# A mixture-of-experts block: routing steps ordered by expert, scatters set between the gathers

## The reference

```python
x = layer_norm(DEEPNORM_ALPHA * x + xa, ln2_g, ln2_b)
scores = sigmoid(x2d @ w_router); sel = scores + router_bias      # 512 x 64
# 8 groups of 8 experts: a group's score is the sum of its top two; keep 4 groups
_, top_idx = lax.top_k(sel, TOP_K)                                # 8 experts per token
w = take_along_axis(scores, top_idx); w = w / w.sum(-1) * ROUTED_SCALE
out = swiglu(x_pad[tok], w_exp_gu[e], w_exp_down[e]) * w          # 64 experts, FF 256
routed + swiglu(x2d, w_sh_gu, w_sh_down)                          # shared expert, FF 256
x = layer_norm(DEEPNORM_ALPHA * x + ff, ln3_g, ln3_b)
```

## Time and profile before

| | us |
|---|---|
| median of 3 runs | 2214.76 (2214.06 to 2220.69) |
| the profiled execution | 2217.79 |
| its span, first to last instruction | 2215.7 |
| PE busy | 2015.8 (91%) |
| DVE busy | 790.7 (36%) |
| ACT busy | 471.6 (21%) |
| POOL busy | 344.0 (16%) |

### The profile page before, as it was taken

One profiled execution on the slowest core, in us unless ns is written; L12 is line 12 of the kernel. 1 busy time (PEld: TensorE's weight loads), 2 busy tenths in 40 slices (PEclk: granted clock), 3 DMA queues, 4 the chain that ended last, 5 costly groups with the idle time before them and its releaser, 6 DMA issues.

```text
span 2215.7 us, 26236 instructions
## 1 busy us (share of the span) xinstructions
PE 2015.8 (91%) x10060; PEld 939.5 (42%) x10060; DVE 790.7 (36%) x1650; ACT 471.6 (21%) x1045; POOL 344.0 (16%) x415
## 2 busy tenths in 40 slices
PE   7888999999977699999999987699988899999997
PEld 3324434445443244443333333344745444444443
DVE  5998771213268033333223222701265300000012
ACT  2235431100300133333333332211244000000000
POOL 0653250000014311111111112400023000000000
PEclk9998999999998799999999999899999999999999
DMA  5110014213222599999999995804310122222210
GB/s 222 47 38 1 10 59 168 76 38 119 110 96 100 193 398 396 403 399 392 391 396 390 392 382 201 316 14 143 124 39 1 63 79 77 76 76 76 76 38 29
DMA packets 67619, 367.91 MB, mean 166 GB/s; under 512 B 11200, under 2 KB 11456, under 8 KB 50784
## 3 DMA queue, kind: packets, MB, share of 16 engines
q1 hardware_dynamic: 44496, 297.76, 35.6%
q10 hardware_dynamic: 10192, 35.57, 4.3%
q0 software_dynamic: 12864, 33.67, 4.2%
HBM read 345.93 MB, written 29.42 MB: 169 GB/s over the span
## 4 chain that ended last, share of the span: by engine, by line
PE 69%; DMA 14%; DVE 10%; issue 4%; POOL 2%; ACT 1%; POOLq 0%; SPq 0%; DVEq 0%; ACTq 0%
PE bank L911 41%; DMA slab<-w_exp_down 12%; PE bank L1231 12%; PE bank L1435 6%; PE bank L920 2%; DVE slab L1846 2%; POOL slot_table L2538 2%; PE bank L1297 2%; DVE slab L1849 1%; PE bank L1249 1%; DVE work L1843 1%; DVE s5x L1846 1%; PE bank L973 1%; DVE slab L1843 1%; PE bank L1193 1%
## 5 line engine op out<-in xcount | busy, mean ns | idle before, releaser
L911 PE MATMUL bank<-slab,ring 128*128 128x512 f32 (+1 forms) x1552 | 660.0, 586 | 13.1 <-DMA ring<-stream 11.4
L911 PEld LDWEIGHTS bank<-slab,ring 128*128 128x128 f32 x1552 | 294.2, 191 | 372.3 <-issue 369.7
L911 PE MATMUL bank<-ring,slab 128*128 128x512 f32 (+1 forms) x608 | 252.8, 576 | 3.9 <-ACT slab L1468 2.1
L1231 PE MATMUL bank<-slab 128*32 128x512 f32 x1536 | 226.1, 593 | 21.3 <-DMA ring<-w_exp_down 15.3
L1231 PE MATMUL bank<-ring,slab 128*32 128x512 f32 x1536 | 227.4, 596 | 18.0 <-DMA slab<-w_exp_down 14.9
L1846 DVE TENSOR_TENSOR slab<-bank,slab 96x256 f32<-96x256 f32 (+3 forms) x120 | 63.8, 531 | 468.8 <-PE bank L911 296.1
L2273 DVE COPY slab<-bank 32x512 f32<-32x512 f32 x124 | 80.9, 688 | 407.6 <-PE bank L1239 407.6
L1239 PE MATMUL bank<-ring,slab 128*32 128x512 f32 x512 | 225.7, 594 | 0.0
L1239 PE MATMUL bank<-slab 128*32 128x512 f32 x480 | 211.6, 594 | 0.0
L2486 POOL TENSOR_TENSOR small<-small 128x1 f32<-128x1 f32 (+2 forms) x30 | 24.0, 801 | 989.9 <-DVE small L1843 989.7
L911 PEld LDWEIGHTS bank<-ring,slab 128*128 128x128 f32 x608 | 115.5, 191 | 137.8 <-issue 129.7
(11 more groups left out here) (263 smaller groups left out, 2185.6 us busy)
## 6 DMA issues: line engine op xcount, KB each, us to landing
ring<-stream SPq DMA_DIRECT2D x173, 512.0 KB, 3.5
slab<-w_exp_gu SPq DMA_DIRECT2D x32, 2048.0 KB
ring<-w_exp_gu SPq DMA_DIRECT2D x32, 2048.0 KB
ring<-w_exp_down SPq DMA_DIRECT2D x32, 1024.0 KB
slab<-w_exp_down SPq DMA_DIRECT2D x32, 1024.0 KB
y_rows<-slab ACTq DMA_DIRECT2D x64, 384.0 KB
gb<-rows ACTq DMA_DIRECT2D x7, 512.0 KB, 5.7
slab<-x_fm SPq DMA_DIRECT2D x1, 2048.0 KB, 9.3
```

The source lines that it names most:

```text
L911: mm = nc.tensor.matmul(dst, lhs[k], rhs[k], start=(k == 0), stop=(k == len(lhs) - 1))
L1231: mm = nc.tensor.matmul(g_bank[32 * g:32 * g + 32, :], x[:, k, 32 * g:32 * g + 32], w[:, 512 * k:512 * k + 512], start=(k == 0), stop=(k = ...
```

## The change

- `psum_order`, `panel_plan`: `pos` before `su` in VectorE's order; the shared down weights leave the ring and come by one DMA of 1 MB into `work` (`sd_w`).
- Norm 2: VectorE normalizes into `xhat` and takes the moments half by half. TensorE transposes `xhat`, rows 0 to 2 as soon as these are done and rows 3 later, and the gain and bias of norm 2 are applied in the copy of the turned tiles, as per-partition scalars. The row form x2, which is stored for the gathers, gets its affine on VectorE for rows 0, 1 (between the halves) and 2 (after the copies), and on GpSimd for rows 3. SP stores it, and loads the rows of norm 3, instead of ScalarE.
- Logits: each 128x64 result in four products with 32 columns of weights, tile by tile as the copies come, for all four row tiles.
- Routing on VectorE: comparisons over all four row tiles at once (128x256), no index search, the rank of a chosen expert within its token by a scan over the chosen mask (so the eight choices of a token come in the order of expert number, not of score), the table address and the y row are one and the same, expert x 96 + slot. For each rank k one fused compare-and-multiply of 128x256 and one reduction give the four addresses of all row tiles.
- The table is laid out by expert. GpSimd scatters rank 0 (four DMAs), then rank k+1 before the gather of expert k, for eight ranks. SP reads the index column of expert e, 96 entries of 4 bytes, by a DMA of its own: for experts 0 to 7 once rank e has been scattered, then in the loop four experts ahead, behind the refills.
- The shared down product comes after the last expert and before the sums.

```diff
@@ SP
-            panels_done(4, 8)
-            gate_up_rows(1, 1)
-            panels_done(8, 10)
-            down_rows(0, 0)
+            def index_column(e):
+                sp.wait_ge(ids_sent[e], 16 * NT)
+                sp.dma_start(slot_tok[:, e % 4:e % 4 + 1], scratch["tab"][e * CAP:(e + 1) * CAP, :]).then_inc(idx_landed[e % 4], 16)
+            sp.dma_start(sd_w, a["w_sh_down"]).then_inc(in_sd, 16)          # after xo
+            early = [(0, 4, lambda: gate_up_rows(0, 0)), (4, 8, lambda: gate_up_rows(1, 1)),
+                     (8, 10, lambda: down_rows(0, 0)), (10, 12, lambda: down_rows(1, 1))]
+            # those whose ring slots hold sg and su (4-8, 8-10) are late, the others go out now
...
+            for t in range(NT):          # wait for x2_dve or x2_pool, then
+                sp.dma_start(scratch["x2"][t * P:(t + 1) * P, :], tm(x2, t)).then_inc(x2_stored, 16)
...
+            down_rows(2, 2)
+            down_rows(3, 3)
+            index_column(0)
+            index_column(1)
+            for x in late:
+                panels_done(*x[:2])
+                x[2]()
             sp.wait_ge(psum_full, plan.full("su", 1))
             gate_up_rows(3, 3)
+            index_column(2)
+            index_column(3)
             for e in range(4):
                 refill(e, e, down=e >= 2)
+                index_column(e + 4)
             with sp.Fori(1, NE // 4 - 1) as u:
                 for b in range(4):
                     refill(4 * u + b, b)
+                    sp.dma_start(slot_tok[:, b:b + 1], scratch["tab"][bass.ds((4 * u + b + 4) * CAP, CAP), :]).then_inc(idx_landed[b], 16)
@@ TensorE
+            for k in range(KD):
+                evac("x2T", k)
+                for t in range(NT):
+                    for g in range(4):
+                        mm = nc.tensor.matmul(tile("lg", t)[32 * g:32 * g + 32, 0:64], fm(x2T, k)[:, t * P + 32 * g:t * P + 32 * g + 32],
+                                              w_rt[:, k, :], start=(k == 0), stop=(k == KD - 1))
...
+                nc.tensor.matmul(dst[:, 0:320], cst("tri"), chosen, start=True, stop=False)
+                for s in range(NT):
+                    n = NT - s
+                    mm = nc.tensor.matmul(dst[:, 64 * s + 64:320].rearrange("p (t e) -> p t e", e=64), ones_f[:, :],
+                                          chosen[:, 64 * s:64 * s + 64].unsqueeze(1).broadcast_to([P, n, 64]),
+                                          start=False, stop=(s == NT - 1))
@@ VectorE
+            link(nc.vector.tensor_tensor_scan(rank, keep_run, chosen[:, 0:256], 0.0, ALU.mult, ALU.add))
+            link(tt(rankm, rank, chosen[:, 0:256], ALU.mult))
+            full("pos", 0)
+            link(ts(ovn, cnt, 1.0 / CAP, -(0.5 + 0.5 / CAP), ALU.mult, ALU.add))
...
+            stt(v3(cmp_a), v3(pos), CAP - 0.5, b64(detour), ALU.is_gt, ALU.mult)
+            tt(v3(cmp_b), v3(pos), b64(place), ALU.add).then_inc(dve_evac, 1)
+            link(tt(yrow, cmp_a, cmp_b, ALU.add))
+            def pick(k, src):
+                return mark(stt(picked[k % 3], rankm, k + 1.0, src, ALU.is_equal, ALU.mult))
+            for k in range(TOPK):
+                m = pick(k + 1, yrow) if k + 1 < TOPK else None
+                dve.wait_ge(dve_step, n)
+                nc.vector.tensor_reduce(yrow_i[:, 4 * k:4 * k + 4], v3(picked[k % 3]), AX, ALU.max).then_inc(route_addr, 1)
+                n = m
+            shared_hidden(0)
+            # the same picks from score into wk, eight, then shared_hidden(1)
@@ GpSimd
+            link(nc.gpsimd.tensor_tensor(tm(x2, 3), tm(xhat, 3), gb[:, 0:D], ALU.mult))
+            nc.gpsimd.tensor_tensor(tm(x2, 3), tm(x2, 3), gb[:, D:2 * D], ALU.add).then_inc(x2_pool, 1)
+            def scatter_ids(k):
+                pool.wait_ge(route_addr, k + 1)
+                for t in range(NT):
+                    pool.indirect_dma_start(scratch["tab"], bass.IndirectOffsetOnAxis(ap=yrow_i[:, 4 * k + t:4 * k + t + 1].bitcast(U32), axis=0),
+                                            tok_i[:, t:t + 1], None).then_inc(ids_sent[k], 16)
+            scatter_ids(0)
+            pool.wait_ge(x2_stored, 16 * NT)
+            for e in range(TOPK):
+                if e + 1 < TOPK:
+                    scatter_ids(e + 1)
+                gather(e // 4, e % 4, e)
```

More of the change, by code:

```diff
@@ L44 @@
 NBLK = NE + NOV
-TABW = 112
 FF = 256
@@ L2171, in _ @@
             shared_hidden(0)
-            full("pos", 0)
-            nc.vector.tensor_copy(cnt, tile("pos", 0)[:, 256:320])
-            nc.vector.tensor_copy(pos_sb, tile("pos", 0)[:, 0:256]).then_inc(dve_evac, 1)
-            dve.wait_ge(dve_evac, plan.done("pos", 0))
-            link(ts(ovn, cnt, CAP + 0.5, None, ALU.is_gt))
-            for q in range(2, T // CAP + 1):
-                link(stt(ovn, cnt, q * CAP + 0.5, ovn, ALU.is_gt, ALU.add))
-            link(nc.vector.memset(cmp_a, 0.0))
@@ new lines, in _ @@
+            n, done = pick(0, score), []
+            for k in range(TOPK):
+                if k >= 2:
+                    dve.wait_ge(dve_step, done[k - 2])
+                m = pick(k + 1, score) if k + 1 < TOPK else None
+                dve.wait_ge(dve_step, n)
+                done.append(mark(nc.vector.tensor_reduce(wk[:, 4 * k:4 * k + 4], v3(picked[k % 3]), AX, ALU.add)))
+                n = m
+            dve.wait_ge(dve_step, done[-1])
+            shared_hidden(1)
+            link(nc.vector.tensor_reduce(wsum, wk.rearrange("p (k t) -> p t k", t=4), AX, ALU.add))
@@ L2557, in _ @@
-            gather(0, 0, True)
-            gather(0, 1, True)
-            with pool.Fori(1, NE // 2) as u:
-                gather(u, 0)
-                gather(u, 1)
+            pool.wait_ge(psum_full, plan.full("xo", 3))
+            nc.gpsimd.memset(slab6[:, :], 0.0)
+            nc.gpsimd.memset(none64, 0.0)
+            nc.gpsimd.memset(chosen[:, 256:320], 0.0)
+            link(nc.gpsimd.memset(keep_run, 1.0))
+            link(nc.gpsimd.memset(keep_run[:, 0:256:64], 0.0))
+            nc.gpsimd.tensor_copy(spare, half_pi).then_inc(route_init, 1)
@@ L2562, in _ @@
+            scatter_ids(0)
+            pool.wait_ge(x2_stored, 16 * NT)
+            for e in range(TOPK):
+                if e + 1 < TOPK:
+                    scatter_ids(e + 1)
+                gather(e // 4, e % 4, e)
+            link(nc.gpsimd.memset(spare, 0.0))
+            nc.gpsimd.tensor_copy(spare, minus_half[:, 0:1]).then_inc(idx_ready, 1)
+            with pool.Fori(TOPK // 4, NE // 4) as u:
+                for b in range(4):
+                    gather(u, b)
             pool.wait_ge(route_ctrl, 2)
```

307 lines of the change are left out of this document (158 added, 149 removed).

## The result

| | before | after |
|---|---|---|
| median, us | 2217.73 (2214.06 to 2224.75, 4 runs) | 2252.06 (2250.33 to 2254.42, 4 runs) |
| profiled execution, us | 2217.79 (span 2215.7) | 2250.33 (span 2248.5) |

The change makes the kernel slower: ratio 1.0152, 95% interval 1.0121 to 1.0182. Forecast were 2163 us and a range up to 2189. This is rival 3's side, to which the prediction gave 0.04, though at 34 us and not at 58.

What follows compares the result with a forecast made beforehand. DMA was taken to bound the expert loop, whose end follows its first refill. Earlier refill -61.8, index columns +6 and shared down product +4 gave -52: 2166 profiled, 2163 us median; range 2148 to 2189.

Steps and rivals of the forecast that it cites:

- rival 3: Expert loop: each index column stops SP's weights for its whole 1.94 us landing, +116, total 2273 us; chance 0.04.
- Index columns in the loop: Expert loop: 60 more small transfers paid in full as DMA time, 4 to 27 us, taken as +6.
- column 2 of the start: Before the loop: its index read queues behind 5 MB of weights, lands near 686; gather 2 may slip 2 us.
- Expert 0's start: Start of the expert loop: expert 0's first product at 682.7 instead of 744.08; first refill 61.8 us earlier.
- norm 2: Before the router: the normalization ends at 637.7 instead of 643.15.
- the mask's own steps: Routing on VectorE: building the mask of chosen experts takes 8.3 us instead of 13.9.
- gather 1's landing: Before expert 0: the gather of expert 1's rows lands 3.9 us after its issue, at 681.7, and sets the start.
- SP's queue: First experts: weights behind the new waits still come in time, with 5 to 13 us of cover.
- The shared down product: Behind the last expert: 13.9 us of product moved there, partly covered by idle time, costs +4.

Runs made afterwards that it cites:

- k6: k3 with eight index columns instead of four, each read eight experts ahead of its gather in the same queue: 2191.09 us, ratio 0.9872.
- k8: k5 plus one index-column read per expert that no instruction uses and nobody waits for until the end: 2200.52 us, ratio 0.9912.
- k14: The changed kernel with index columns 2 to 63 read by GpSimd on its own queue, nothing else changed: 2184.86 us, ratio 0.9838.
- k13: The changed kernel with SP holding the late weights (5 MB) until gathers 0 and 1 have landed: 2263.05 us, ratio 1.0198.
- k3: k1 with the shared down product back ahead of the expert loop: 2214.96 us, ratio 0.9986.
- k1: The changed kernel with each loop index column issued before expert e's refill instead of behind it: 2220.34 us, ratio 1.0009.
- k4: k3 with logits in 64 records of 128 columns, testing whether TensorE ran out of fetched instructions in the gap: 2216.25 us, one run.
- k11: k3 with columns from 2 on read on GpSimd's own queue, plus logits in 64 records of 128 columns: 2175.67 us, ratio 0.9806.
- k12: k11 plus late weights held until gathers 0 and 1 have landed: 2174.44 us, ratio 0.9793.
- k7: k3 with index columns from expert 8 on read by GpSimd on its own queue, behind the gather before: 2183.36 us, ratio 0.9835.
- k5: k3 with the table read at once in 3 transfers and columns copied in SBUF from expert 8 on: 2198.14 us, ratio 0.9903.

## Why the prediction was wrong

**The step that failed** is *Index columns in the loop*: "60 more transfers ... so they are paid in full". It priced what a column costs the DMA engines, and k6 and k8 put that price at 5 to 9 us (forecast 6). It did not ask when a column lands and who waits: 11.6 us after an issue that had no lead over its gather, which made +70.4 of the +6. The wait was new and in plain sight in the diff (`idx_landed` ahead of each gather), and the queue ahead of it as well: SP issues the column right behind 3 MB. The working was even done for column 2 of the start ("queues behind them and lands near 686"), and not carried into the loop. With rows of before it could have been: 3 MB at 388 GB/s are 8 us, a gather 3.9 on idle queues, a turn 1.5, a product 9, together 22 us in a circle of three experts, 7.5 each; every 3 us that the column and the gather take longer under load add 1 to that, against a pace of 9.2 to 9.8. Both landings were known only from an idle stretch. That should have made it a rival of weight.

**Rival 3** had the sign and the wrong mechanism: a column does not stop the weights. 70.4 us over 60 columns is 1.2 each, near its 1.0 of decision, but by chance: the same columns cost little when they are read eight ahead (k6), or from another queue and 25 us ahead (k14).

By the Trainium skill (DMA: Bandwidth & Descriptors, "Queues, rings and completion order") each of the 16 engines takes one ring's descriptors in ring order, and changes between the rows of different issuers packet by packet. The traces agree: 11.6, 18.2 and 30.0 us behind growing stocks of weights in SP's ring, 9.2 in GpSimd's. By the same page of the Trainium skill ("Rules for kernel authors") spreading DMAs over the issuing engines does nothing for bandwidth. The traces agree, 388 GB/s before and 394 in k14; what differs by queue is how long a small transfer takes to land.

**Expert 0's start** was forecast at 682.7 and came at 696.7. 6 of it is gather 1's issue (683.4 against 677.5), which comes from the first scatter (665.35 against 658.7): norm 2 (637.0 against 637.7) and the mask's own steps (7.8 against 8.3) were right; the gap in the logits (5.4) is the greater part. The other 8 is gather 1's landing, priced at 3.9 by the earlier trace rows where nothing else moved; beside 5 MB of weights it took 11.8, and k13 shows that these are the cause. *SP's queue* had asked whether the weights come in time, and never what they do to a gather.

**The shared down product** was about right (+6.3 in the trace, forecast +4; k3 against k1 gives 5.4 by the medians, not resolved). What was forecast for the whole, -52, stands against about -33 for k14's span (2183.1 against 2215.7): with the columns mended, expert 0's start (694.6, 12 late) is most of what is left, and first to last refill took 569.5 us against 560.3 before, +9 where +6 was forecast.

**Open:** what makes the 5.4-us gap in the 32-column records. The profile shows no semaphore that TensorE waits for there, but its DMA queues give a hint that speaks for k4's theory I. In all twelve kernels with this form one packet of 0.02 MB of the queue for instructions (q8) moves within the gap, between 643 and 646 us, while SP's queue holds 95 to 99% of the engines (638 to 649 us), and TensorE goes on some 2 us later. The three kernels with 128 columns (k4, k11, k12) have no such packet from 638 to 649 us and no gap. No run takes the weights away from there, so the cause isn't shown. Nor does a run change only the queue of the columns, or only their lead with the queue of k14. What the held weights would bring with columns on GpSimd's queue and the shared down product behind the loop wasn't tried.

## What to carry to other kernels

For each transfer that is added, ask for two prices: what it takes from the engines, and how long it stands in its queue with someone waiting; the second is set by the bytes ahead of it, not by its own. Compare it with the lead: how long before its use the transfer can be issued. Put a small transfer that gates work on a queue without bulk traffic, or issue it so far ahead that its landing no longer matters. When one wait feeds the next issue, write the circle down, add it up and divide by its steps, since only this shows that it is longer than the engine's own pace.

## What the runs showed of the hardware

- 0.4 KB behind weights on one queue landed in 11.6, 18.2 and 30.0 us (changed kernel, k1, k6), each time about as long as the 1 MB of down weights in the same queue (11.8 to 12.4, 18.0 to 18.5, 30.4 to 30.6); on GpSimd's queue in 9.2 (k7). The table's 42 KB on an idle queue took 1.9 before.
- A gather of 96 rows took 3.9 us alone and 8.9 to 11.8 beside the weights, even on its own queue.
- A 4-byte packet in SP's queue costs some 15 to 24 ns of one engine where nobody waits for it (k6; k8 against k5), a rough figure. On GpSimd's queue a column shows as about 32 packets: 7835 less 14.59/15.92 of before's 6720, over 53 reads.
- 203 records with 32-column weights ran at 15 ns each and were followed by 5.1 to 5.4 us without one, in all twelve kernels of this form; 64 of 128 columns took 7.54 us without a gap (k4, k11, k12).
